# Middle FFN's up projection: block products from its seventh pair on, with the scaled input rewritten by blocks

## The chip, the cores and the metric

One Trainium2 chip, of which the kernel uses one core. The metric is the device time of one execution in microseconds (us). Five engines matter here: TensorE (PE) multiplies matrices, VectorE (DVE) and ScalarE (ACT) work element by element, GpSimd (POOL) does too, and SyncE (SP) issues the loads of the weights. Each engine runs its own instructions in program order and waits for others at semaphores.

## The reference, cut to what matters

The program is two transformer blocks in a row over 512 tokens of width 1024. The second block, `second_block`, begins and ends with a gated feed-forward network. The one in the middle of the whole program (`ffn1`) is the one that changes:

```
h = rms_norm(x, ffn1_norm)
x = x + 0.5 * (silu(h @ w_gate) * (h @ w_up)) @ w_down
```

Here `w_gate` and `w_up` have 2816 columns each, 22 chunks of 128. `ffn2`, the last one, has the same form. All is fp32.

## The kernel before, in words

The activations lie with features on partitions and tokens along the free dimension: `u_hi` and `u_lo` are 8 chunks of 128 features by 512 tokens. Every fp32 value is split into a rounded part (`_hi`, type fp32r) and the rest (`_lo`), and every product is three matmuls: hi by hi, lo by hi, hi by lo.

Weights stream in slabs of 128x1024. SP loads a slab into `raw` (four of them), ACT rounds it into `w_hi` (L1759), POOL subtracts to get `w_lo` (L880), and PE waits for that subtraction before the first matmul of a slab. There are five slab places in `w_hi` and `w_lo`, and ACT's function `feed_to` rounds slabs ahead in its own program order, between its other work.

The three up projections are called `up`, `up1` and `up2`. Each works in 22 pairs: pair c is chunk c of the gate and chunk c of the value. In the plain form a pair is two groups of 8 feature chunks, 48 matmuls of 128x512. So group 2c is pair c's gate and group 2c+1 its value, and group g of `up1` uses slab g of that layer. The first two pairs (four groups) go side by side.

In `up2` the last 18 pairs take another form, which the text calls a block pair. The 1024 by 512 input is cut into 2 by 2 blocks, the pair's weights too, and seven half-size products replace eight (`paired`, 7 products of 12 matmuls, 84 matmuls of 128x256). The products need four sums of input blocks (`s_all`, rounded to `s_hi` on ACT, their rest `s_lo` on POOL), made once, and for every pair seven weight pieces: three raw quarters (pieces 0, 2 and 6), and four differences (pieces 1, 3, 4, 5; in the code `pair_two`, `pair_three`, `pair_one`, `pair_four`). POOL makes the difference of piece 3 (`t_three`, in `slot[5]`) and the rests of pieces 0, 2, 3 and 6. DVE makes the other differences and rests. ACT rounds all seven. Between the products DVE adds partial results (`slot[4]`, `slot[2]`, `slot[3]`, semaphore `st_out`), on which later products of the pair wait; ACT copies the first partial result aside (L2001, semaphore `st_first`) before product 2.

The input of a block pair must be scaled by the norm's factor first, since sums of blocks are taken of it. The layer begins before that factor is known: its first pairs run on the unscaled input, and DVE multiplies their results by the factor `r_sb` (L2675, L2681). In `up2`, DVE scales the input (`scale_input`, L2610), ACT and DVE rewrite `u_hi` and `u_lo`, and DVE makes the block sums (`input_sums`, L2628), all while PE computes the first pairs. In `up1` all 22 pairs are plain, and the input is never scaled.

In both gated layers of the second block, DVE multiplies the silu of the gate by the value (L2684), ACT rounds the product into `a_hi` (L1940) and DVE subtracts to get `a_lo` (L2670). For late chunks of a layer with block pairs the product is kept in `a_kept` instead, and split near the end of the layer.

Of the kernel before, what the change touches and what calls it, by code (L numbers as in the profile page):

```python
# [113 lines left out]
PAIRED = {"up2": (4, FC)}  # L114
# [4 lines left out]
SUM_ORDER = (1, 2, 0, 3)  # L119
# [83 lines left out]
def build(nc, t):  # L203

    ctx = ExitStack()
    with ctx:  # L206
# [609 lines left out]
        def _(pool):  # L816

            def pair_pool(p):

                def low(i, src, hi):  # L820
                    pool.wait_ge(st_hi, hi_no(p, hi))
                    nc.gpsimd.tensor_tensor(piece(w_lo, p, i), src, piece(w_hi, p, i).bitcast(F32),  # L822
                                            ALU.subtract).then_inc(st_pool, 1)

                wait_raw(pool, p, 0)
                wait_raw(pool, p, 1)
                name, c = PAIRS[p]
# [12 lines left out]
                low(6, raw_half(p, 1, 1), 7)  # L840
# [45 lines left out]
        def _(pe):  # L886
# [78 lines left out]
            def dense(name, src_hi, src_lo, k_ready=None, after=None, row=None, row_at=None, again=None, upto=None,  # L965
# [56 lines left out]
                for m in range(ahead, upto or n):  # L1022
                    g = g0 + m
                    wait_bank(g)
                    out = psum[bank_of[g]][:, :]
                    for i in range(k):
                        row_step(m, i)
                        hi, lo = weight(tile)
                        if k_ready and m == 0:
                            pe.wait_ge(k_ready[0], k_ready[1] + i + 1)  # L1030
                        if again is not None and m == ahead:
                            pe.wait_ge(u_ready, again + i + 1)
                        x_hi, x_lo = sources(i)
                        first = mm(out, hi, x_hi, start=(i == 0), stop=False)  # L1034
                        if m == last_reads and i >= 1:
# [9 lines left out]
            def paired(name, scaled):  # L1045
# [17 lines left out]
                for c in range(*PAIRED[name]):  # L1063
# [8 lines left out]
                    if first_pair:  # L1072
                        pe.wait_ge(u_ready, scaled + 4)
# [7 lines left out]
                    if first_pair:  # L1081
                        pe.wait_ge(u_ready, scaled + 8)
# [13 lines left out]
                    pe.wait_ge(st_out, 5 * p + 2)  # L1096
                    product(p, 5, y, "a22", False)
# [621 lines left out]
            dense("up1", u_hi, u_lo, (u_ready, 4 * DC), row="pre2", row_at=(4, 4))  # L1719
            dense("down1", a_hi, a_lo, (a_ready, FC))  # L1720
            dense("wq", u_hi, u_lo, (u_ready, 5 * DC), row="pre3", row_at=(0, 2), again=6 * DC)
# [19 lines left out]
            dense("up2", u_hi, u_lo, (u_ready, 7 * DC), row="pre4", row_at=(0, 2), again=8 * DC, upto=8)  # L1741
            paired("up2", 8 * DC)
# [6 lines left out]
        def _(act):  # L1749
# [186 lines left out]
            def ffn_swiglu(n, name, paired_from=FC, paired_to=FC, unscaled=FC):  # L1936
# [24 lines left out]
                for c in range(paired_from):  # L1961
                    if c == 3 and unscaled == paired_from:
                        for i in range(4):
                            sum_hi_of(name, i)
                    if c == paired_from - 2:
                        pair_raw(p, 0)
                    if c == paired_from - 1:
                        pair_raw(p, 2)
                        pair_three(p)
                        pair_two(p)  # L1970
                        pair_one(p)
                        pair_four(p)
                    silu_of(c)
                    if c == paired_from - 1:
                        pair_raw(p, 6)
                        pair_raw(p + 1, 0)
                        if unscaled == paired_from:
                            for i in range(DC):
                                act.wait_ge(ux_done, DC + 4 + i + 1)
                                if i < DC - 1:  # L1980
                                    act.wait_ge(u_read, DC - 2 + i + 1)
                                else:
                                    act.wait_ge(dense_done, group_of(name, 2 * c + 1))
                                f(u_hi[:, i, :], u_all[:, i, :], ACT.Copy).then_inc(u_part, 1)
                    if 1 <= c <= KEPT_FROM:
                        rounded_a(c - 1)
# [369 lines left out]
            ffn_swiglu(1, "up1")  # L2356
            late_act(3, 24, "mix2", "wq", "down1")
            rewrite_hi(DC + 4, "wq", DC - 2, [slot[4][:, :], slot[5][:, :]])
# [173 lines left out]
            rewrite_hi(2 * DC + 4, "up2", 2 * (DC - 2), [u_all[:, c, :] for c in range(DC)], sums=True)  # L2532
# [5 lines left out]
        def _(dve):  # L2538
# [127 lines left out]
            def ffn_gate(n, name, paired_from=FC, paired_to=FC, unscaled=FC):  # L2666
# [29 lines left out]
                for c in range(paired_from):  # L2696
# [9 lines left out]
                    if c == paired_from - 1 and unscaled == paired_from:  # L2706
                        input_lo(5 * DC)
# [28 lines left out]
                for c in range(paired_from, paired_to):  # L2736
# [17 lines left out]
                    if more:  # L2754
# [11 lines left out]
                    if more:  # L2766
# [4 lines left out]
                    TT(slot[3][:, 0:256], y, kept, ALU.add).then_inc(st_out, 1)  # L2771
                apart(12, 13)
# [433 lines left out]
            ffn_gate(1, "up1")  # L3206
            add_half("down1", 0.5, "pre3", ("mix2", 5 * DC))
            inverse("pre3")
            rewrite("mix2", 6 * DC, r_sb, slot[4:6])
# [190 lines left out]
            add_half("out", 0.5, "pre4", ("ffn2", 7 * DC))  # L3400
            inverse("pre4")
            scale_input("ffn2")
            input_lo(8 * DC)
            input_sums("up2", 3 * DC + 4)
# [162 lines left out]
```

## Time and profile before

| what | value |
|---|---|
| median of 3 runs | 2148.84 us (2148.69 to 2149.2) |
| the profiled execution's own time | 2148.84 us |
| span that its profile shows | 2147.0 us |
| PE busy | 2122.9 us, 99% of the span |
| DVE, ACT, POOL busy | 1009.2, 941.7 and 948.3 us, 44 to 47% |

The span is 1.84 us shorter than the profiled execution's time, which is the median of the runs. A timeline row is: start in us from the span's start, duration in us, engine, line, operation, what it writes and reads, shape, count of instructions merged into the row, and in brackets the idle time of its engine before it and who ended it. PE's matmuls overlap each other, so their pace is read from their starts.

### The profile page before, as it was taken

The page shows a single profiled execution, that of the slowest core. Times are in us where ns is not written, and L with a number is a line of the kernel's source. Part 1 is how long each engine was busy: PE and PEld are TensorE (multiplying, and loading weights), DVE is VectorE, ACT ScalarE, POOL GpSimd, SP SyncE. Part 2 cuts the span into 40 slices and gives each one's busy share as a digit, 9 for nine tenths or more (in the row PEclk, how much of TensorE's full clock was granted, in tenths as well). Part 3 has the DMA queues.
Part 4 walks back from the last instruction along what each step waited for, and adds up shares of the span by engine and source line. Part 5 has one row for each costly group of instructions (what it writes and reads, how often), then busy time and mean ns, then how long its engine had stood idle before and what let it go on. Part 6 is the DMA issues. An engine that isn't in the chain of part 4 may idle for free. (4 is left out here: it accounts for less than half of the span.)

```text
span 2147.0 us, 29183 instructions
## 1 busy us (share of the span) xinstructions
PE 2122.9 (99%) x11584; PEld 1775.0 (83%) x11584; DVE 1009.2 (47%) x1821; ACT 941.7 (44%) x1629; POOL 948.3 (44%) x441
## 2 busy tenths in 40 slices
PE   9999999999999999999999999999999999999998
PEld 8788877787888888888888888778888887999986
DVE  7684555446655400563332124653744127776611
ACT  7835545545544422442223222762346234545521
POOL 4423322345544543654444344143524445766631
PEclk9999999999999999999999999999999999999999
DMA  4313321232332332223333233023322332333321
GB/s 179 97 50 113 112 66 50 104 112 79 108 97 94 114 98 88 89 89 98 98 94 102 89 98 104 21 87 99 111 81 68 98 98 79 99 101 113 117 93 49
DMA packets 56439, 200.68 MB, mean 93 GB/s; under 512 B 6640, under 2 KB 7536, under 8 KB 55920
## 3 DMA queue, kind: packets, MB, share of 16 engines
q1 hardware_dynamic: 52416, 188.77, 27.7%
q10 hardware_dynamic: 3888, 10.05, 1.4%
q8 instruction: 92, 1.51, 0.3%
q14 instruction: 43, 0.35, 0.1%
HBM read 194.60 MB, written 2.10 MB: 92 GB/s over the span
## 5 line engine op out<-in xcount | busy, mean ns | idle before, releaser
L880 POOL TENSOR_TENSOR w_lo<-raw,w_hi 128x1024 fp32r<-128x1024 f32 x313 | 770.0, 2472 | 1013.6 <-ACT w_hi L1759 985.7
L1759 ACT ACTIVATE w_hi<-raw 128x1024 fp32r<-128x1024 f32 x316 | 326.7, 1051 | 146.9 <-PE dense L1038 84.7
L1034 PE MATMUL dense<-u_hi,w_hi 128*128 128x512 f32 x608 | 237.4, 391 | 0.6 <-ACT slot L1950 0.6
L1038 PE MATMUL dense<-u_hi,w_lo 128*128 128x512 f32 x608 | 236.6, 389 | 0.0
L1037 PE MATMUL dense<-u_lo,w_hi 128*128 128x512 f32 x584 | 227.2, 389 | 0.0
L1034 PE MATMUL dense<-a_hi,w_hi 128*128 128x512 f32 x400 | 156.0, 390 | 0.0
L1037 PE MATMUL dense<-a_lo,w_hi 128*128 128x512 f32 x400 | 155.6, 389 | 0.0
L1038 PE MATMUL dense<-a_hi,w_lo 128*128 128x512 f32 x400 | 155.6, 389 | 0.0
L1034 PE MATMUL misc<-u_hi,w_hi 128*128 128x512 f32 x368 | 143.6, 390 | 0.7 <-DVE u_lo L2616 0.7
L1038 PE MATMUL misc<-u_hi,w_lo 128*128 128x512 f32 x368 | 143.2, 389 | 0.0
L1037 PE MATMUL misc<-u_lo,w_hi 128*128 128x512 f32 x360 | 140.1, 389 | 0.0
L1034 PEld LDWEIGHTS dense<-u_hi,w_hi 128*128 128x128 f32 x608 | 114.1, 188 | 25.3 <-ACT slot L1950 1.1
L1038 PEld LDWEIGHTS dense<-u_hi,w_lo 128*128 128x128 f32 x608 | 114.1, 188 | 23.8
L1037 PEld LDWEIGHTS dense<-u_lo,w_hi 128*128 128x128 f32 x584 | 109.6, 188 | 22.8
L2784 DVE SCALAR_TENSOR_TENSOR h<-dense,h 128x512 f32<-128x512 f32 x24 | 16.6, 692 | 212.9 <-PE dense L1038 212.9
L822 POOL TENSOR_TENSOR w_lo<-raw,w_hi 128x512 fp32r<-128x512 f32 x54 | 70.1, 1313 | 56.2 <-ACT w_hi L1765 56.2
L1037 PEld LDWEIGHTS dense<-a_lo,w_hi 128*128 128x128 f32 x400 | 75.1, 188 | 15.9 <-issue 0.2
L1034 PEld LDWEIGHTS dense<-a_hi,w_hi 128*128 128x128 f32 x400 | 75.1, 188 | 15.7 <-issue 0.2
L1038 PEld LDWEIGHTS dense<-a_hi,w_lo 128*128 128x128 f32 x400 | 75.1, 188 | 15.5
L1034 PEld LDWEIGHTS misc<-u_hi,w_hi 128*128 128x128 f32 x368 | 69.1, 188 | 15.8 <-issue 1.5
L958 PE MATMUL misc<-u_hi,w_hi 128*128 128x512 f32 x192 | 81.6, 425 | 0.0
L1038 PEld LDWEIGHTS misc<-u_hi,w_lo 128*128 128x128 f32 x368 | 69.1, 188 | 14.5
(569 smaller groups left out, 5009.3 us busy)
## 6 DMA issues: line engine op xcount, KB each, us to landing
raw<-in_weights SPq DMA_DIRECT2D x352, 512.0 KB, 3.5
h<-in_x SPq DMA_DIRECT2D x4, 512.0 KB, 6.6
alibi<-in_alibi ACTq DMA_DIRECT2D x1, 2048.0 KB, 8.9
h<-in_x ACTq DMA_DIRECT2D x2, 1024.0 KB, 7.2
out<-result SPq DMA_DIRECT2D x8, 256.0 KB, 2.2
p_raw<-in_p ACTq DMA_DIRECT2D x2, 512.0 KB, 3.2
hn<-mqk ACTq DMA_DIRECT2D x4, 256.0 KB, 4.0
mqk<-mqk ACTq DMA_DIRECT2D x4, 256.0 KB, 3.9
```

Of the source, the lines that this page charges most:

```text
L822: nc.gpsimd.tensor_tensor(piece(w_lo, p, i), src, piece(w_hi, p, i).bitcast(F32), ALU.subtract).then_inc(st_pool, 1)
L880: nc.gpsimd.tensor_tensor(w_lo[:, ring(s), :, :], raw[:, s % RAWS, :, :], w_hi[:, ring(s), :, :].bitcast(F32), ALU.subtract).then_inc(w_sp ...
L958: mm(out, hi, src_hi[:, i, :], start=(i == 0), stop=False)
L1034: first = mm(out, hi, x_hi, start=(i == 0), stop=False)
L1037: mm(out, hi, x_lo, start=False, stop=False)
L1038: last = mm(out, lo, x_hi, start=False, stop=(i == k - 1))
L1759: f(w_hi[:, ring(s), :, :], raw[:, s % RAWS, :, :], ACT.Copy).then_inc(w_part, 1)
L2784: STT(h[:, c, :], out_bank(name, c)[:, :], scale, h[:, c, :], ALU.mult, ALU.add).then_inc(h_ready, 1)
```

## The change

The layer `up1` joins `PAIRED`, from pair 6 on: its pairs 0 to 5 stay plain and pairs 6 to 21 become block pairs. What comes with that:

- DVE's `ffn_gate` scales the whole input after pair 1 and makes the block sums after pair 2. ACT's `ffn_swiglu` rounds the four sums after the silu of pair 3.
- The input is rewritten in three blocks, at the end of pair 5: features 0 to 511 of the first 256 tokens (block a11), then features 512 to 1023 of the first and of the second 256 tokens (a12, a22). PE waits for each at the product that reads it first.
- In the first block pair of `up1` DVE takes another order (`late`): the value of pair 5, and the weight differences of the next pair one at a time between the additions.
- POOL's first block pair of a layer, in `up1` and in `up2` alike, takes the four rests of the sums in turns with the weight pieces, where `up2` had them all ahead of the weight pieces.
- ACT rounds the activation of an earlier pair before it rounds the weight pieces of the first block pair.
- `down1` takes the turned order of sources and the banks that `down2` has.

```diff
-PAIRED = {"up2": (4, FC)}
+PAIRED = {"up1": (6, FC), "up2": (4, FC)}
...
-                if c == PAIRED[name][0]:
-                    for i in SUM_ORDER:
-                        pool.wait_ge(st_hi, sum_no(name, i + 1, BLOCKS))
-                        nc.gpsimd.tensor_tensor(s_lo[i][:, :, :], s_all[:, i, :, :], s_hi[i][:, :, :].bitcast(F32),
-                                                ALU.subtract).then_inc(st_slo, 1)
-                else:
+                if not first_pair:
                     pool.wait_ge(st_pool, 5 * p - 1)
                 three = t_three[:, :].rearrange("p (a b) -> p a b", a=4)
                 nc.gpsimd.tensor_tensor(three, raw_half(p, 1, 1), raw_half(p, 1, 0), ALU.subtract).then_inc(st_pool, 1)
                 low(0, raw_half(p, 0, 0), 1)
+                if first_pair:
+                    sum_low(1)
                 low(2, raw_half(p, 0, 1), 2)
+                if first_pair:
+                    sum_low(2)
                 low(3, three, 3)
+                if first_pair:
+                    sum_low(0)
+                    sum_low(3)
                 low(6, raw_half(p, 1, 1), 7)
...
-            dense("up1", u_hi, u_lo, (u_ready, 4 * DC), row="pre2", row_at=(4, 4))
-            dense("down1", a_hi, a_lo, (a_ready, FC))
+            dense("up1", u_hi, u_lo, (u_ready, 4 * DC), row="pre2", row_at=(4, 4), upto=12, last_reads=11)
+            paired("up1", 5 * DC + 1, 5 * DC + 2, 5 * DC + 3)
+            dense("down1", a_hi, a_lo, (a_ready, FC), turned_from=KEPT_FROM)
...
                     if c == paired_from - 1:
+                        if c <= KEPT_FROM:
+                            rounded_a(c - 1)
                         pair_raw(p, 2)
                         pair_three(p)
                         pair_two(p)
                         pair_one(p)
                         pair_four(p)
                     silu_of(c)
+                    if c == 3 and unscaled == paired_from:
+                        for i in range(4):
+                            sum_hi_of(name, i)
                     if c == paired_from - 1:
                         pair_raw(p, 6)
+                        if unscaled == paired_from:
+                            act.wait_ge(ux_done, 2 * DC + 4)
+                            act.wait_ge(u_read, DC - 1)
+                            f(u_hi[:, 0:4, 0:256], u_all[:, 0:4, 0:256], ACT.Copy).then_inc(u_part, 1)
+                            act.wait_ge(dense_done, group_of(name, 2 * c + 1))
+                            for x in (slice(0, 256), slice(256, S)):
+                                f(u_hi[:, 4:8, x], u_all[:, 4:8, x], ACT.Copy).then_inc(u_part, 1)
...
                     if c == paired_from - 1 and unscaled == paired_from:
-                        input_lo(5 * DC)
+                        low_a(c - 1)
+                        for i, (k, x) in enumerate(((0, slice(0, 256)), (4, slice(0, 256)), (4, slice(256, S)))):
+                            dve.wait_ge(u_part, 5 * DC + i + 1)
+                            TT(u_lo[:, k:k + 4, x], u_all[:, k:k + 4, x], u_hi[:, k:k + 4, x].bitcast(F32),
+                               ALU.subtract).then_inc(u_ready, 1)
+                        break
...
                     TT(slot[4][:, 0:256], y, kept, ALU.add).then_inc(st_out, 1)
-                    if more:
+                    late = c == paired_from == unscaled
+                    if late:
+                        value_of(c - 1)
+                    elif more:
                         pair_one(p + 1)
                         pair_two(p + 1)
...
-            ffn_gate(1, "up1")
+            ffn_gate(1, "up1", *PAIRED["up1"], PAIRED["up1"][0])
```

The order of instructions moves at three places.

On ACT in `up1`, between the silu of pair 3 (it writes `slot1` from `dense0`) and that of pair 4. Before:

```order
L1950 ACTIVATE slot1_62<-dense0 128x512 [waits a_ready,up_scaled]
L1940 ACTIVATE a_hi_142<-slot0_61 128x512 [waits a_raw]
L1759 ACTIVATE w_hi_50<-raw_49 128x1024 [waits dense_done,w_loaded1]
L1759 ACTIVATE w_hi_50<-raw_49 128x1024 [waits dense_done,w_loaded2]
L1950 ACTIVATE slot0_61<-dense2 128x512 [waits a_ready,up_scaled]
```

With the change:

```order
L1961 ACTIVATE slot1_62<-dense0 128x512 [waits a_ready,up_scaled]
L1808 ACTIVATE s_hi0_147<-s_all_146 128x1024 [waits st_diff]
L1808 ACTIVATE s_hi1_148<-s_all_146 128x1024 [waits st_diff]
L1808 ACTIVATE s_hi2_149<-s_all_146 128x1024 [waits st_diff]
L1808 ACTIVATE s_hi3_150<-s_all_146 128x1024 [waits st_diff]
L1951 ACTIVATE a_hi_142<-slot0_61 128x512 [waits a_raw]
L1776 ACTIVATE w_hi_50<-raw_49 128x512 [waits dense_done,w_loaded3]
L1770 ACTIVATE w_hi_50<-raw_49 128x1024 [waits dense_done,w_loaded1]
L1770 ACTIVATE w_hi_50<-raw_49 128x1024 [waits dense_done,w_loaded2]
L1961 ACTIVATE slot0_61<-dense2 128x512 [waits a_ready,up_scaled]
```

The two whole slabs are those of groups 10 and 11. They now stand behind the four sums and one weight quarter of the first block pair.

On DVE in `up1`, from the product of pair 1 (`slot1` by `dense3`) to the gate of pair 3 (`dense0`). Before:

```order
L2684 TENSOR_TENSOR slot1_62<-slot1_62,dense3 128x512 [waits up_act,dve_step]
L2670 TENSOR_TENSOR a_lo_143<-slot0_61,a_hi_142 128x512 [waits a_part]
L2675 TENSOR_TENSOR misc0<-misc0,r_sb_155 128x512 [waits dense_done]
L2681 TENSOR_TENSOR misc1<-misc1,r_sb_155 128x512 [waits dense_done]
L2684 TENSOR_TENSOR slot0_61<-slot0_61,misc1 128x512 [waits up_act,dve_step]
L2670 TENSOR_TENSOR a_lo_143<-slot1_62,a_hi_142 128x512 [waits a_part]
L2675 TENSOR_TENSOR dense0<-dense0,r_sb_155 128x512 [waits dense_done]
```

With the change:

```order
L2696 TENSOR_TENSOR slot1_62<-slot1_62,dense3 128x512 [waits up_act,dve_step]
L2622 SCALAR_TENSOR_TENSOR u_all_145<-h_52,vec_56,r_sb_155 128x512 x8
L2682 TENSOR_TENSOR a_lo_143<-slot0_61,a_hi_142 128x512 [waits a_part]
L2687 TENSOR_TENSOR misc0<-misc0,r_sb_155 128x512 [waits dense_done]
L2693 TENSOR_TENSOR misc1<-misc1,r_sb_155 128x512 [waits dense_done]
L2696 TENSOR_TENSOR slot0_61<-slot0_61,misc1 128x512 [waits up_act,dve_step]
L2640 TENSOR_TENSOR s_all_146<-u_all_145 128x1024 [waits ux_done]
L2640 TENSOR_TENSOR s_all_146<-s_all_146,u_all_145 128x1024 [waits st_diff]
L2640 TENSOR_TENSOR s_all_146<-u_all_145 128x1024
L2640 TENSOR_TENSOR s_all_146<-u_all_145,s_all_146 128x1024 [waits st_diff]
L2682 TENSOR_TENSOR a_lo_143<-slot1_62,a_hi_142 128x512 [waits a_part]
L2687 TENSOR_TENSOR dense0<-dense0,r_sb_155 128x512 [waits dense_done]
```

The gate of pair 3, on which ACT's silu of pair 3 waits, now stands behind eight scalings and four sums.

On POOL at the start of `up2`'s block pairs, from the end of the plain slabs to the difference `slot5` of the second block pair (pair 5). Before:

```order
L831 TENSOR_TENSOR s_lo1_152<-s_all_146,s_hi1_148 128x1024 [waits st_hi,w_loaded3,w_loaded2]
L831 TENSOR_TENSOR s_lo2_153<-s_all_146,s_hi2_149 128x1024 [waits st_hi]
L831 TENSOR_TENSOR s_lo0_151<-s_all_146,s_hi0_147 128x1024 [waits st_hi]
L831 TENSOR_TENSOR s_lo3_154<-s_all_146,s_hi3_150 128x1024 [waits st_hi]
L836 TENSOR_TENSOR slot5_66<-raw_49 128x512
L822 TENSOR_TENSOR w_lo_51<-raw_49,w_hi_50 128x512 [waits st_hi] x2
L822 TENSOR_TENSOR w_lo_51<-slot5_66,w_hi_50 128x512 [waits st_hi]
L822 TENSOR_TENSOR w_lo_51<-raw_49,w_hi_50 128x512 [waits st_hi]
L836 TENSOR_TENSOR slot5_66<-raw_49 128x512 [waits st_pool,w_loaded1,w_loaded0]
```

With the change:

```order
L837 TENSOR_TENSOR slot5_66<-raw_49 128x512 [waits w_loaded3,w_loaded2]
L821 TENSOR_TENSOR w_lo_51<-raw_49,w_hi_50 128x512 [waits st_hi]
L831 TENSOR_TENSOR s_lo1_152<-s_all_146,s_hi1_148 128x1024 [waits st_hi]
L821 TENSOR_TENSOR w_lo_51<-raw_49,w_hi_50 128x512 [waits st_hi]
L831 TENSOR_TENSOR s_lo2_153<-s_all_146,s_hi2_149 128x1024 [waits st_hi]
L821 TENSOR_TENSOR w_lo_51<-slot5_66,w_hi_50 128x512 [waits st_hi]
L831 TENSOR_TENSOR s_lo0_151<-s_all_146,s_hi0_147 128x1024 [waits st_hi]
L831 TENSOR_TENSOR s_lo3_154<-s_all_146,s_hi3_150 128x1024 [waits st_hi]
L821 TENSOR_TENSOR w_lo_51<-raw_49,w_hi_50 128x512 [waits st_hi]
L837 TENSOR_TENSOR slot5_66<-raw_49 128x512 [waits st_pool,w_loaded1,w_loaded0]
```

The first difference moved to the head, and every rest of a sum now stands behind the rest of piece 0, which waits for ACT to round that piece.

## Rows read from the trace of the kernel before

**Rows 1.** The page: busy time by engine, and TensorE's granted clock in 40 slices.

```profile
PE 2122.9 (99%) x11584; PEld 1775.0 (83%) x11584; DVE 1009.2 (47%) x1821; ACT 941.7 (44%) x1629; POOL 948.3 (44%) x441
PEclk9999999999999999999999999999999999999999
```

**Rows 2.** Timeline of PE in `up1`: first matmuls of groups 10 and 11.

```profile
970.19 0.39 PE L1034 MATMUL misc<-u_hi,w_hi 128*128 128x512 f32 x1
...
975.63 0.39 PE L1034 MATMUL misc<-u_hi,w_hi 128*128 128x512 f32 x1
```

**Rows 3.** Timeline of PE in `up2`'s block pairs: first matmuls of pairs, and waits.

```profile
1829.67 0.28 PE L1058 MATMUL dense<-u_hi,w_hi 128*128 128x256 f32 x1
...
1833.84 0.36 PE L1058 MATMUL dense<-u_hi,w_hi 128*128 128x256 f32 x1 [1.13 <-POOL w_lo L822]
...
1840.18 0.35 PE L1058 MATMUL misc<-s_hi,w_hi 128*128 128x256 f32 x1 [0.36 <-issue]
...
1841.68 0.28 PE L1058 MATMUL misc<-u_hi,w_hi 128*128 128x256 f32 x1
...
1850.88 0.36 PE L1058 MATMUL dense<-s_hi,w_hi 128*128 128x256 f32 x1 [0.41 <-DVE slot L2765]
...
1862.47 0.28 PE L1058 MATMUL misc<-u_hi,w_hi 128*128 128x256 f32 x1
...
1872.55 0.28 PE L1058 MATMUL dense<-u_hi,w_hi 128*128 128x256 f32 x1
...
2011.28 0.36 PE L1058 MATMUL dense<-u_hi,w_hi 128*128 128x256 f32 x1 [0.33 <-DVE slot L2753]
```

**Rows 4.** Timeline of DVE in `up1`, from the factor on.

```profile
942.63 0.70 DVE L2675 TENSOR_TENSOR dense<-dense,r_sb 128x512 f32<-128x512 f32 x1 [5.29 <-ACT r_sb L1934]
...
947.25 0.68 DVE L2670 TENSOR_TENSOR a_lo<-slot,a_hi 128x512 fp32r<-128x512 f32 x1
```

**Rows 5.** Timeline of ACT in `up1`.

```profile
949.60 1.05 ACT L1759 ACTIVATE w_hi<-raw 128x1024 fp32r<-128x1024 f32 x1
954.80 0.60 ACT L1950 ACTIVATE slot<-dense 128x512 f32<-128x512 f32 x1 [4.15 <-DVE dense L2675]
...
955.82 2.00 ACT L1759 ACTIVATE w_hi<-raw 128x1024 fp32r<-128x1024 f32 x2
```

**Rows 6.** Timeline of DVE at the start of `up2`.

```profile
1813.22 1.22 DVE L2628 TENSOR_TENSOR s_all<-u_all 128x1024 f32<-128x1024 f32 x1
...
1823.02 2.90 DVE L2639 TENSOR_TENSOR misc<-raw 128x512 f32<-128x512 f32 x1
...
1837.33 0.68 DVE L2655 TENSOR_TENSOR w_lo<-misc,w_hi 128x512 fp32r<-128x512 f32 x1
1838.11 0.70 DVE L2650 TENSOR_TENSOR misc<-raw,misc 128x512 f32<-128x512 f32 x1
1838.72 1.03 DVE L2670 TENSOR_TENSOR a_lo<-slot,a_hi 128x512 fp32r<-128x512 f32 x1
```

**Rows 7.** Timeline of POOL at the start of `up2`.

```profile
1814.57 10.79 POOL L831 TENSOR_TENSOR s_lo<-s_all,s_hi 128x1024 fp32r<-128x1024 f32 x4 [8.42 <-ACT s_hi L1797]
...
1833.23 1.74 POOL L836 TENSOR_TENSOR slot<-raw 128x512 f32<-128x512 f32 x1
...
1842.54 2.57 POOL L822 TENSOR_TENSOR w_lo<-raw,w_hi 128x512 fp32r<-128x512 f32 x2
```

**Rows 8.** Timeline of ACT at the start of `up2`.

```profile
1821.03 0.62 ACT L1765 ACTIVATE w_hi<-raw 128x512 fp32r<-128x512 f32 x1
...
1833.36 0.38 ACT L2001 ACTIVATE slot<-dense 128x256 f32<-128x256 f32 x1
1835.00 0.63 ACT L1765 ACTIVATE w_hi<-slot 128x512 fp32r<-128x512 f32 x1 [1.26 <-POOL slot L836]
```

**Rows 9.** DVE's line that scales the input: duration ns as min/median/max.

```profile
L2610 DVE SCALAR_TENSOR_TENSOR u_all<-h,vec,r_sb x8: 739/750/2905, 1790.3 to 1801.4; 128x512 f32<-128x512 f32 x8
```

**Rows 10.** POOL's line for a plain slab: duration ns as min/median/max.

```profile
L880 POOL TENSOR_TENSOR w_lo<-raw,w_hi x313: 2340/2399/3311, 7.4 to 2109.0; 128x1024 fp32r<-128x1024 f32 x157
```

More of the change, by code:

```diff
@@ L118 @@
 SUM_AT = (2, 0, 1, 3)
-SUM_ORDER = (1, 2, 0, 3)
 def first_slab(name, c):
@@ L1034, in dense @@
                         first = mm(out, hi, x_hi, start=(i == 0), stop=False)
-                        if m == last_reads and i >= 1:
+                        if m == last_reads and i == 4:
                             first.then_inc(u_read, 1)
@@ L1096, in paired @@
                     pe.wait_ge(st_out, 5 * p + 2)
+                    if first_pair:
+                        pe.wait_ge(u_ready, a22_ready)
                     product(p, 5, y, "a22", False)
@@ L1740, in _ @@
             dense("out", mg_hi, mg_lo, (mg_ready, 0))
-            dense("up2", u_hi, u_lo, (u_ready, 7 * DC), row="pre4", row_at=(0, 2), again=8 * DC, upto=8)
-            paired("up2", 8 * DC)
+            dense("up2", u_hi, u_lo, (u_ready, 7 * DC + 3), row="pre4", row_at=(0, 2), again=8 * DC + 3, upto=8)
+            paired("up2", 8 * DC + 7, 8 * DC + 11, 8 * DC + 11)
             dense("down2", a_hi, a_lo, (a_ready, 2 * FC), row="pre5", row_at=(DC - 1, FC - 2), turned_from=KEPT_FROM)
@@ L1961, in ffn_swiglu @@
                 for c in range(paired_from):
-                    if c == 3 and unscaled == paired_from:
-                        for i in range(4):
-                            sum_hi_of(name, i)
                     if c == paired_from - 2:
@@ L1973, in ffn_swiglu @@
                     silu_of(c)
+                    if c == 3 and unscaled == paired_from:
+                        for i in range(4):
+                            sum_hi_of(name, i)
                     if c == paired_from - 1:
                         pair_raw(p, 6)
-                        pair_raw(p + 1, 0)
[L1977 to L1985, printed above, removed]
+                        if unscaled == paired_from:
[5 more added lines that the diff above has]
+                                f(u_hi[:, 4:8, x], u_all[:, 4:8, x], ACT.Copy).then_inc(u_part, 1)
+                        pair_raw(p + 1, 0)
+                    elif 1 <= c <= KEPT_FROM:
                         rounded_a(c - 1)
@@ L2355, in _ @@
             late_act(2, 16, "ffn1", "up1")
-            ffn_swiglu(1, "up1")
+            ffn_swiglu(1, "up1", *PAIRED["up1"], PAIRED["up1"][0])
             late_act(3, 24, "mix2", "wq", "down1")
-            rewrite_hi(DC + 4, "wq", DC - 2, [slot[4][:, :], slot[5][:, :]])
+            rewrite_hi(2 * DC + 4, "wq", DC - 1, [slot[4][:, :], slot[5][:, :]])
             act.dma_start(wvb[:, :], t["wvb"]).then_inc(c_loaded, 16)
@@ L2531, in _ @@
             late_act(4, 32, "ffn2", "up2", "out")
-            rewrite_hi(2 * DC + 4, "up2", 2 * (DC - 2), [u_all[:, c, :] for c in range(DC)], sums=True)
+            rewrite_hi(3 * DC + 4, "up2", 2 * DC - 3, [u_all[:, c, :] for c in range(DC)], sums=True)
             ffn_swiglu(2, "up2", *PAIRED["up2"], 2)
@@ L2753, in ffn_gate @@
                     TT(slot[4][:, 256:S], y, kept, ALU.add).then_inc(st_out, 1)
-                    if more:
+                    if late:
+                        pair_one(p + 1)
+                    elif more:
                         pair_two_lo(p + 1)
@@ L2765, in ffn_gate @@
                     TT(slot[2][:, 256:S], z, slot[4][:, 256:S], ALU.add).then_inc(st_out, 1)
-                    if more:
+                    if late:
+                        pair_two(p + 1)
+                    elif more:
                         pair_four_lo(p + 1)
@@ L2771, in ffn_gate @@
                     TT(slot[3][:, 0:256], y, kept, ALU.add).then_inc(st_out, 1)
+                    if late:
+                        pair_two_lo(p + 1)
+                        pair_four(p + 1)
+                        pair_four_lo(p + 1)
                 apart(12, 13)
@@ L3205, in _ @@
             inverse("pre2")
-            ffn_gate(1, "up1")
-            add_half("down1", 0.5, "pre3", ("mix2", 5 * DC))
+            ffn_gate(1, "up1", *PAIRED["up1"], PAIRED["up1"][0])
+            add_half("down1", 0.5, "pre3", ("mix2", 5 * DC + 3))
             inverse("pre3")
-            rewrite("mix2", 6 * DC, r_sb, slot[4:6])
+            rewrite("mix2", 6 * DC + 3, r_sb, slot[4:6])
             for c in range(8):
@@ L3399, in _ @@
                 TT(mg_lo[:, m, :], ma[:, m, :], mg_hi[:, m, :].bitcast(F32), ALU.subtract).then_inc(mg_ready, 1)
-            add_half("out", 0.5, "pre4", ("ffn2", 7 * DC))
+            add_half("out", 0.5, "pre4", ("ffn2", 7 * DC + 3))
             inverse("pre4")
             scale_input("ffn2")
-            input_lo(8 * DC)
-            input_sums("up2", 3 * DC + 4)
+            input_lo(8 * DC + 3)
+            input_sums("up2", 4 * DC + 4)
             ffn_gate(2, "up2", *PAIRED["up2"], 2)
```

13 lines of the change are left out of this document (9 added, 4 removed).

## Prediction, made before the changed kernel ran

> **What bounds the kernel now.** I read the page first: PE is busy for 99% of the span, and its granted clock is at full speed, 2.4 GHz, in every slice [rows 1]. So only two things can change the time: the sum of PE's own pace, and new waits of PE. Then I read PE's timeline in `up1`, the layer that changes, for its pace: a group of 24 matmuls goes from 970.19 to 975.63, which is 5.44 us or 226.7 ns a matmul, and a plain pair takes 10.88 us [rows 2]. Then I read PE's timeline in `up2`, which already has block pairs. Undisturbed, a pair goes from 1862.47 to 1872.55: 10.08 us for 84 matmuls, 120 ns each [rows 3]. The reader should see there that the first pairs do not reach this: the first takes 12.01 us (1829.67 to 1841.68), with restarts at 1833.84 (product 2) and 1840.18 (product 6). The second waits once (1850.88) and so does the last (2011.28) [rows 3]. Last I read DVE, ACT and POOL around both places, since a layer that enters block pairs asks much of these three in a short time, and each works strictly in program order.
>
> **What is removed.** Sixteen pairs go from 10.88 to 10.08 us: 16 x 0.80 = 12.8 us [rows 2, 3]. The Trainium skill ("TensorE: Matmul & The Clock Gate", section on the back-to-back issue gap) gives N/2.4 + 2.5 ns for a matmul of N columns on a warm engine. By that page a plain pair would be an estimated 10.36 us and a block pair 9.17, and sixteen would give 19 us. No row here has either pace, and the sum goes by the rows. Also gone are DVE's multiplications by the factor for these pairs, off PE's path.
>
> **Added wait 1: the slab of group 10.** I carry the times of the trace on. DVE is free for the scaling at 947.25 [rows 4]. POOL has nothing to do then, since ACT's next slab now comes only after the silu of pair 2. Eight scalings at 0.75 us [rows 9], less about 0.08 each for overlap with the next start, end at 952.6. A rest, the gate and the value of pair 2 (four operations of some 0.7 us [rows 4]) end at 955.3. Then come four block sums of 1.22 us [rows 6], about 4.8 us. But ACT's slab of group 9 now starts at 955.0 and POOL's 2.40 us for it [rows 10] fall into these sums. When both engines read SBUF only, one waits for the other: the first difference on DVE at 1823.02 took 2.90 us [rows 6], while POOL's first operations took 1.74 us where the later ones go in 2.57 for two [rows 7]. So I add 2.0 us, and with one more rest and the gate of pair 3 DVE is at 963.35. ACT follows with the silu (0.60), four roundings of the sums at some 1.0, two half-size ones at 0.5 and the slab of group 10 at 1.05 [rows 5, 8]: 969.85. POOL's 2.40 us end at 972.3. PE wanted group 10 at 970.19 [rows 2]. That is 2.1 us, plus 0.1 for the restart: **2.2 us**. The bounds are 0.2 (POOL's slab beside the sums costs nothing) and 2.8.
>
> **Added wait 2: the first block pair of `up1`.** Group 11 now ends at 981.07 + 2.2 = 983.3. Until then the chain is: POOL's slab of group 11 to 974.9, its first difference to 976.6 (1.74 [rows 7], beside a rest of DVE); ACT rounds pieces 3 and 1 (977.7); DVE's rest and difference 5, 0.7 each [rows 6]; ACT rounds it (979.7); DVE's rest and the gate of pair 5 (981.1); ACT's silu, one quarter, and then block a11 of the input, 1.05, ready at 983.2. The rest of a11 on DVE takes 1.22 alone, and 2 us behind one of POOL's, which has the rests of the sums in hand then. Product 0 starts at 985.2, **1.9 late** (bounds 1.2 and 2.4). After it DVE has a12 and a22, each behind an operation of POOL (1.25, then 2.4), then a rest of a weight piece and the first addition, for which product 3 waits: about 991.8, where 985.2 + 36 x 0.12 = 989.5 would do. **2.3 late** (bounds 0 and 3).
>
> **Added waits 3: second and last pair.** `late` leaves the next pair's piece 1, 5 and 4 to the end of the first pair. By the same count the first addition of pair 7 comes 0.65 late, about what the second pair of `up2` lost (1850.88 [rows 3]); bounds 0 and 2. The last pair has the code of `up2`'s last, and I take its wait: the gap before 2011.28 cost some 0.6 [rows 3].
>
> **POOL's turns, in `up2` too.** Before, POOL did the four rests of the sums from 1814.57 to 1825.36, while ACT was still busy with pairs 0 and 1 [rows 7]. Now they stand behind the rest of piece 0, and ACT rounds piece 0 at 1821.03 to 1821.65 [rows 8], after two silus and an activation; nothing in the change moves that. So POOL makes its first difference early and then stands idle until 1821.7. From there it has four rests of sums (2.36 each, between the shortest and the median of a plain slab [rows 10]) and, to the end of the second pair's difference, five half-size operations (1.25 from start to start): 15.7 us, and 1.9 more for four collisions with DVE at 0.45 (1.74 less 1.3 [rows 7]). It ends at 1839.3. Before, that second difference ended at 1833.23 + 1.74 = 1834.97 [rows 7].
>
> What waits for it: ACT rounds it (at 1835.00 in the trace [rows 8]), and behind that row stand an activation, the silu and piece 1 of the second pair. DVE then has the rest of piece 1, difference 5, a rest of an activation, and only then the addition that product 6 of the first pair waits for [rows 6]. From the end of that difference to product 6 the trace has 1840.18 - 1834.97 = 5.2 us [rows 3, 7]. Some 0.4 of it was a wait for PE, so I take 4.8. Product 6 starts at 1844.1 and the pair ends 12 x 0.12 later, 1845.5, against 1841.68: **3.9 us lost**. In return the early difference cures the wait at 1833.84, which the view puts on POOL, but which ended with ACT's copy at 1833.36 + 0.38 [rows 3, 8]; that is in these numbers already. Bounds: no collisions and 4.6 us of chain give 1.8; the full 5.2 and one more collision give 4.9. I take 3.9, since collisions are the rule in these rows.
>
> **The sum.** -12.8 + 2.2 + 1.9 + 2.3 + 0.65 + 0.6 + 3.9 = -1.2 us. The span of 2147.0 becomes 2145.8; with the 1.84 us around it 2147.6, and the profiled execution is the median, so **2147.6 us** it is for the median too. The turned sources and banks of `down1`, the counts of the later layers, and the loads cost nothing: the same instructions stand there, and two slabs per 10.08 us are what `up2` streams. ACT's earlier activation is in the chains above.
>
> **Rivals.** Measured against no change, 0.2% (4.3 us) is about what the measurement can tell.
>
> *POOL's turns do not hold `up2` up.* If product 6 came on time, `up2` would lose nothing and gain its 1.9 us of first waits: -12.8 + 7.7 - 1.9 = -7.0, 2141.8 us. It needs the second difference by about 1833.5; the order of POOL's rows speaks against it. A kin of it is that the collisions hardly count, on both layers: lower bounds 0.2 + 1.2 + 0 + 0 + 0.6 and 1.8 give -9.0, 2139.8. Together 0.33.
>
> *`up1` never catches up, and the kernel is slower.* DVE begins the second block pair behind. If every further pair of `up1` kept the 0.65 us of the second, 14 x 0.65 = 9.1 us come on top: 2156.7. The point from which it decides is whether DVE needs over 10.08 us for a pair's work. Against it: `up2` is in step from its third pair on [rows 3]. For it: the first pair hands on more work than in `up2`. Chance 0.12.
>
> *A block pair at the page's pace.* The Trainium skill's rule for the gap (the same section) would make the gain 19 us. As a mechanism of this kernel it would mean that block matmuls in `up1` start every 109 ns and plain ones every 216, which gives -19 + 11.6 = -7.4, 2141.4 us. `up2`'s identical matmuls at 120 ns leave it 0.02.
>
> **The numbers.** The forecast's case has 0.53, and its own range is 2144.5 to 2151, where the waits' upper bounds (0.6, 1.2, 1.35 and 1.0 us more) would not all meet. The range for 8 in 10 reaches down into the first rival, 2140.5, and up to 2152. Faster by over 0.2% (below 2144.5) 0.36, within 0.2% 0.50, slower (above 2153.1) 0.14.
>
> **What would show it.** Block pairs of `up1` from its third on at 10.08 us; a gap of PE before group 10 that ends with POOL's slab; gaps before products 0 and 3 of the first block pair, ended by DVE's rest of the input and first addition; in `up2`, POOL idle before 1821.7 on the old axis, no gap before product 2, and one of some 6 us before product 6. I am wrong if PE does not stop before group 10 or product 6, or if later pairs of `up1` stop too.

## The result, and the profile after

The changed kernel takes 2152.34 us (median of 15 runs, 2151.67 to 2154.07), the kernel before 2149.2 us on the same chip: a ratio of 1.0015, 95% interval 1.0008 to 1.0022. That is 3.1 us slower, where the forecast of 2147.6 us was a little faster, and 0.3 us above its range. By the bound of 0.2% it is no change.

The page of the changed kernel, by engine (busy us, share of the span, instructions):

```profile
PE 2115.0 (98%) x12160; PEld 1795.3 (83%) x12160; DVE 1105.2 (51%) x1996; ACT 987.2 (46%) x1748; POOL 993.6 (46%) x493
```

PE is busy for 7.9 us less than in [rows 1], so the block products do save work; the waits took more than that back. PE's timeline in `up1`, first matmul behind each wait (start, duration, and in brackets the idle time and who ended it):

```profile
973.79 0.47 PE L1042 MATMUL misc<-u_hi,w_hi 128*128 128x512 f32 x1 [1.52 <-POOL w_lo L888]
...
986.59 0.36 PE L1066 MATMUL dense<-u_hi,w_hi 128*128 128x256 f32 x1 [1.67 <-DVE u_lo L2722]
993.05 0.36 PE L1066 MATMUL dense<-s_hi,w_hi 128*128 128x256 f32 x1 [1.91 <-issue]
1003.08 0.36 PE L1066 MATMUL misc<-u_hi,w_hi 128*128 128x256 f32 x1 [1.17 <-ACT slot L2013]
...
1149.08 0.36 PE L1066 MATMUL dense<-u_hi,w_hi 128*128 128x256 f32 x1 [0.33 <-DVE slot L2773]
```

These are, in order, group 10, product 0 and product 3 of the first block pair, product 2 of the second and product 2 of the last. Between the second and the last, each pair takes 10.08 us. The same for `up2`, from the second group of its start to the second block pair:

```profile
1806.14 0.51 PE L1042 MATMUL misc<-u_hi,w_hi 128*128 128x512 f32 x1 [0.67 <-DVE u_lo L2628]
...
1836.94 0.28 PE L1068 MATMUL dense<-u_hi,w_lo 128*128 128x256 f32 x1
1842.84 0.55 PE L1066 MATMUL misc<-s_hi,w_hi 128*128 128x256 f32 x1 [5.62 <-POOL w_lo L821]
1843.19 0.42 PE L1067 MATMUL misc<-s_lo,w_hi 128*128 128x256 f32 x1
1843.41 0.42 PE L1068 MATMUL misc<-s_hi,w_lo 128*128 128x256 f32 x1
```

No wait stands ahead of product 2 any more (1833.84 in [rows 3]), and a wait of 5.6 us stands ahead of product 6. Behind it the starts lie 213 ns apart, not 120. The table of windows shows why (length, PE busy and its matmuls, granted clock as a share of 2.4 GHz, DMA):

```profile
1836.90:1842.80 5.90, 0.32 (x3) 0.86 0.31 95
1842.80:1848.00 5.20, 5.16 (x24) 0.50 0.57 195
1848.10:1853.00 4.90, 4.90 (x43) 1.00 0.02 3
```

In the wait the granted clock falls to 0.50, its level of 1.2 GHz (half clock, below), and it stays there for 24 matmuls. The page's row of the clock in 40 slices shows 9 throughout, as in [rows 1]: 5 us vanish in a slice of 54. The Trainium skill ("TensorE: Matmul & The Clock Gate", section on HAM oscillation) says that an engine left idle between bursts of matmuls comes back at half rate; this trace agrees, with 0.50 behind 5.6 us.

What held product 6 is read from POOL, ACT and DVE:

```profile
1803.80 1.74 POOL L837 TENSOR_TENSOR slot<-raw 128x512 f32<-128x512 f32 x1
1820.52 1.42 POOL L821 TENSOR_TENSOR w_lo<-raw,w_hi 128x512 fp32r<-128x512 f32 x1 [14.98 <-ACT w_hi L1776]
1821.90 2.85 POOL L831 TENSOR_TENSOR s_lo<-s_all,s_hi 128x1024 fp32r<-128x1024 f32 x1
...
1830.04 5.67 POOL L831 TENSOR_TENSOR s_lo<-s_all,s_hi 128x1024 fp32r<-128x1024 f32 x2
1835.66 1.31 POOL L821 TENSOR_TENSOR w_lo<-raw,w_hi 128x512 fp32r<-128x512 f32 x1
1836.91 1.28 POOL L837 TENSOR_TENSOR slot<-raw 128x512 f32<-128x512 f32 x1
```

```profile
1838.22 0.63 ACT L1776 ACTIVATE w_hi<-slot 128x512 fp32r<-128x512 f32 x1 [7.74 <-POOL slot L837]
```

```profile
1842.33 0.41 DVE L2787 TENSOR_TENSOR slot<-misc,slot 128x256 f32<-128x256 f32 x1
```

POOL stands idle for 15 us behind its first difference, does the sums afterwards, and comes to the second pair's difference at 1836.91. ACT rounds that at 1838.22, and DVE's addition for product 6 ends at 1842.74. The view names POOL, but POOL's rest of piece 6 had ended at 1836.97 (1835.66 + 1.31). DVE's addition ended 0.1 us before product 6 started, so that addition, at the end of POOL's chain, is what was late.

The start of `up2` lost too. At 1803.80 POOL's first difference meets DVE's rests of the input (L2628), and the group at 1806.14 waits for one of them. The second rest takes 1.77 us beside POOL, and those behind it 0.68. Below is DVE's row there, merged over four rests, 5.38 us:

```profile
1801.91 5.38 DVE L2628 TENSOR_TENSOR u_lo<-u_all,u_hi 128x512 fp32r<-128x512 f32 x4 [2.09 <-ACT u_hi L1873]
```

Against the trace before, PE's starts are 1.95 us later when `up1` begins, 3.03 earlier at `down1`, 2.51 earlier at `wq`'s second group, 2.31 earlier at `up2` and 4.55 later at its third block pair. The 1.95 arise ahead of `up1`: 1.5 of them are matmuls at half clock behind a 1.9 us wait at 222 us. The ten profiles of the experiments have that wait too, one of them with 2.2 us, and none has the half clock there.

### The profile page after: what moved, and what is told of

The parts are those of the page before. It is cut to its first block and busy times, and to the rows that moved or that the text cites. A ratio compares the mean times of both kernels' runs of the same rounds, so it can differ in the third digit from the quotient of the medians.

```text
span 2151.6 us, 30943 instructions
## 1 busy us (share of the span) xinstructions
PE 2115.0 (98%) x12160; PEld 1795.3 (83%) x12160; DVE 1105.2 (51%) x1996; ACT 987.2 (46%) x1748; POOL 993.6 (46%) x493
## 5 line engine op out<-in xcount | busy, mean ns | idle before, releaser
L888 POOL TENSOR_TENSOR w_lo<-raw,w_hi 128x1024 fp32r<-128x1024 f32 x281 | 695.6, 2487 | 920.1 <-ACT w_hi L1770 892.3
L821 POOL TENSOR_TENSOR w_lo<-raw,w_hi 128x512 fp32r<-128x512 f32 x102 | 131.4, 1302 | 116.1 <-ACT w_hi L1776 116.1
L1042 PE MATMUL dense<-u_hi,w_hi 128*128 128x512 f32 x432 | 168.9, 391 | 0.8 <-ACT slot L1961 0.8
L1046 PE MATMUL dense<-u_hi,w_lo 128*128 128x512 f32 x432 | 168.1, 389 | 0.0
L1045 PE MATMUL dense<-u_lo,w_hi 128*128 128x512 f32 x408 | 158.7, 389 | 0.0
L1066 PE MATMUL dense<-s_hi,w_hi 128*128 128x256 f32 x408 | 115.7, 284 | 2.0 <-issue 1.9
L1042 PE MATMUL misc<-u_hi,w_hi 128*128 128x512 f32 x288 | 112.7, 391 | 2.9 <-POOL w_lo L888 1.5
L1067 PE MATMUL dense<-s_lo,w_hi 128*128 128x256 f32 x408 | 115.4, 283 | 0.0
L1068 PE MATMUL dense<-s_hi,w_lo 128*128 128x256 f32 x408 | 115.4, 283 | 0.0
L1046 PE MATMUL dense<-a_lo,w_lo 128*128 128x512 f32 x256 | 99.6, 389 | 0.0
```

The costliest lines, as they stand in the source:

```text
L888: nc.gpsimd.tensor_tensor(w_lo[:, ring(s), :, :], raw[:, s % RAWS, :, :], w_hi[:, ring(s), :, :].bitcast(F32), ALU.subtract).then_inc(w_sp ...
L1066: mm(out, hi[:, k, :], a_h[:, k, :], start=(start and k == 0), stop=False, skip_group_check=True)
L1067: mm(out, hi[:, k, :], a_l[:, k, :], start=False, stop=False, skip_group_check=True)
L1068: last = mm(out, lo[:, k, :], a_h[:, k, :], start=False, stop=(k == 3), skip_group_check=True)
```

## The experiments

Theory: `up1` does what was forecast, and POOL's turns in `up2` cost more than forecast, by the half clock behind the wait (2.25 us) and by the collision at the start of `up2` (0.95). Rivals: the clock fell for a reason of its own, or the wait comes from the new code in general and not from POOL's order. All ratios are to the kernel before, which had 2149.19 to 2149.33 us beside them.

**Old order in `up2`.**

```diff
+                turns = first_pair and name == "up1"
                 if not first_pair:
                     pool.wait_ge(st_pool, 5 * p - 1)
+                elif not turns:
+                    for i in (1, 2, 0, 3):
+                        sum_low(i)
...
-                if first_pair:
+                if turns:
                     sum_low(1)
```

> The changed kernel with POOL's order of before in up2 alone (its four sum remainders ahead of the first difference); up1 keeps the turns. Theory (POOL's turns in up2 cost 0.95 us at the start of up2, about 3.6 us of a longer wait at product 6 of the first block pair and 2.25 us of matmuls at half clock behind that wait): 2145.6 us, product 2 of that pair waits again, product 6 hardly, and no stretch at a granted clock of 0.50. Rival A (the clock falls there for another reason than the wait): 2147.9. Rival B (the wait at product 6 is due to the new code around up1 and the sums, not to the order on POOL): 2152.

Measured: 2145.87 us, ratio 0.9983 (0.9974 to 0.9991), 6.5 us below the changed kernel. The waits of PE in `up2` (total, times, longest):

```profile
PE dense L1070 <- POOL w_lo L821: 1.3, 1, 1.3
PE misc L1070 <- issue: 0.8, 1, 0.8
PE misc L1046 <- DVE u_lo L2632: 0.7, 1, 0.7
PE dense L1046 <- ACT slot L1965: 0.6, 1, 0.6
```

Product 2 waits again and product 6 for 0.8 us only; DVE's rests take 5.49 us for six where the changed kernel had 5.38 for four. So the theory holds for `up2`, and with POOL's old order there the change is 3.3 us faster than the kernel before.

**The turns alone.** The kernel before, with the new `pair_pool` and nothing else.

```diff
-                if c == PAIRED[name][0]:
-                    for i in SUM_ORDER:
...
+                if first_pair:
+                    sum_low(1)
                 low(2, raw_half(p, 0, 1), 2)
```

> The kernel before with POOL's turns in up2 and nothing else of the change. Theory: it loses what up2 lost in the changed kernel, 0.95 + 5.8 us, so 2155.9 us against 2149.2, with the same 5.6 us wait at product 6 and the same stretch at half clock. Rival A (the start of up2 was late because of the phase in which the changed kernel reaches it, not because of POOL's early difference): 2155.0. Rival B (the turns cost little by themselves): 2149 to 2150.

Measured: 2155.0 us, ratio 1.0028 (1.0018 to 1.0039), 5.8 us slower. Its trace loses 1.07 us from `up2`'s first matmul to its first block pair, 5.11 in that pair, and gets 0.22 back in the second. The time is Rival A's number, but the start of `up2` does lose what Rival A excludes; the theory's 2155.9 was 0.9 too high in all. Here the half clock ends after some 14 matmuls where the changed kernel had 24 (columns as above):

```profile
1844.60:1848.00 3.40, 3.05 (x14) 0.51 0.68 195
```

**No idle time ahead of product 6.** Added matmuls fill the wait, into a bank that nobody reads.

```diff
                     product(p, 5, y, "a22", False)
+                    if first_pair and name == "up2":
+                        idle = pair_banks(p + 1)[2]
+                        pe.wait_ge(*last_before_pairs[name][idle])
+                        spare = psum[idle][:, 0:256]
+                        for _ in range(42):
+                            mm(spare, piece(w_hi, p, 5)[:, 0, :], u_hi[:, 4, second], start=True, stop=True,
+                               skip_group_check=True)
```

> The changed kernel, and in the wait ahead of product 6 of up2's first block pair PE runs 42 matmuls of 128x256 into a bank that nobody reads (42 x 0.120 = 5.0 us of a wait of 5.6 us). They compute nothing that is used. Theory (the granted clock falls to 0.50 because PE stands idle): product 6 starts as late as before, 14.4 us after its pair, but its matmuls and those behind it run at 1.00 and the time is 2.2 us less than that of the changed kernel, 2150.1. Rival A (the clock falls at that place whatever PE does): no gain, 2152.3. Rival B (PE's extra reads slow POOL or DVE down, or the 42 matmuls end later than the wait): 2152.5 or more.

Measured: 2150.39 us, ratio 1.0005 (0.9997 to 1.0014), 1.95 us below the changed kernel. Product 6 starts 14.51 us after its pair, 0.1 later than in the changed kernel, and the window behind it shows:

```profile
1841.20:1846.40 5.20, 5.10 (x42) 1.00 0.56 196
```

42 matmuls where the changed kernel had 24. This experiment took nothing away but PE's idleness, so the idleness is what brought the half clock, and neither rival holds. From the first pair's start to the third's, the trace takes 26.4 us instead of 28.5. All five profiles with a wait of 5.6 us there and no added matmuls (the changed kernel, the turns alone and the next three with POOL's turns in `up2`) have half clock behind it, for 14 to 30 matmuls.

**`down1`'s banks of before.**

```diff
-        for name in PAIRED:
-            for m in range(DC):
-                bank_of[START["down" + name[2:]][1] + m] = (2, 3, 0, 1)[m % 4]
+        for m in range(DC):
+            bank_of[START["down2"][1] + m] = (2, 3, 0, 1)[m % 4]
```

> The changed kernel with down1's groups in the banks of before (0, 1, 2, 3 in turn), down2's as they are. Theory (the last groups of down1 now share banks with the first groups of wq): the first wq groups start 0.5 us earlier against down1, 2151.8 us. Rival (the start of wq hangs on DVE's late input alone, whatever the banks): 2152.3, no difference. Either difference is near what five rounds can tell; the trace's step from down1 to wq decides.

Measured: 2151.72 us, ratio 1.0010 (1.0001 to 1.0018), 0.6 us below, near what the runs can tell. `wq`'s first group starts as before, 119.7 us after `down1`. The gap ahead of its second group is gone, so that one comes 0.5 us earlier (first the changed kernel, then this one; the second row of each is that group):

```profile
1272.05 0.39 PE L1018 MATMUL dense<-u_hi,w_lo 128*128 128x512 f32 x1
1272.77 0.50 PE L1015 MATMUL dense<-u_hi,w_hi 128*128 128x512 f32 x1 [0.33 <-DVE h L2812]
```

```profile
1270.46 0.39 PE L1017 MATMUL dense<-u_hi,w_lo 128*128 128x512 f32 x1
1270.69 0.39 PE L1014 MATMUL dense<-u_hi,w_hi 128*128 128x512 f32 x1
```

**ACT's slabs first.** In `up1`, ACT rounds the slabs of groups 10 and 11 ahead of the four sums.

```diff
                     if c == 3 and unscaled == paired_from:
+                        feed(name, 2 * c + 4)
                         for i in range(4):
                             sum_hi_of(name, i)
```

> The changed kernel with ACT rounding the slabs of up1's groups 10 and 11 ahead of the four input sums, not behind them. Theory (group 10 waits because POOL's remainder of its slab waits for ACT's rounding, which stands behind 4.2 us of sums): group 10 starts 1.6 us earlier against up1's start, and since nothing behind it was late before, the time falls by 0.5 to 1.6 us, to 2150.7 to 2151.8. Rival (ACT then waits for a free place in the ring, and the sums and DVE's work behind them come late): no gain or a loss, 2152 to 2154.

Measured: 2152.37 us, no gain. Group 10 starts 1.69 us earlier against the start of `up1`, and product 0 waits for 4.53 instead of 1.67, so that it starts 1.1 us later. The sums, and the rounding for which DVE waits behind them, come 1.9 us later on ACT. And POOL is through with its slabs sooner, so its first rest of the block pair meets DVE's first difference (POOL, then DVE):

```profile
970.82 1.76 POOL L821 TENSOR_TENSOR w_lo<-raw,w_hi 128x512 fp32r<-128x512 f32 x1
```

```profile
971.35 1.78 DVE L2652 TENSOR_TENSOR misc<-raw 128x512 f32<-128x512 f32 x1
...
973.77 0.69 DVE L2688 TENSOR_TENSOR dense<-dense,r_sb 128x512 f32<-128x512 f32 x1
```

That difference took 0.69 us in the changed kernel. With both losses the gate at 973.77 comes 3.7 us later, of which slack takes up all but the 1.1. The longer wait was also followed by half clock (columns as above):

```profile
986.00:989.50 3.50, 3.48 (x16) 0.51 0.00 0
```

Product 3 then waits for 0.4 us instead of 1.9, and `up1` takes 236.3 us in all, where the changed kernel took 235.9. The rival holds in its outcome. Of its mechanism, the later sums are there and no wait of ACT for a free slab place is; the collision and the half clock it did not name.

**DVE's third rest later.** The rest of a22 is moved behind the first addition (in the code it is item 2 of the loop over the three rests), the value of pair 5 behind the second.

```diff
                     if late:
-                        value_of(c - 1)
+                        low_u(2)
...
                     if late:
+                        value_of(c - 1)
                         pair_one(p + 1)
```

> The changed kernel with DVE's third input remainder of up1's first block pair moved behind the first sum of outputs, and the value of pair 5 behind the second. Theory (product 3 waits 2.2 us for that sum, which stands behind 3.4 us of the third remainder): product 3 waits at most 0.3 us, product 5 waits for the third remainder some 0.3 us in its place, and the time falls by 1.5 to 2 us, to 2150.5. Rival (the third remainder, which product 5 needs, takes over the wait at its full length): 2152.3.

Measured: 2151.74 us, 0.6 us below the changed kernel, a third of what the theory had. The traces don't put those 0.6 down to the edit: `up1` takes 236.0 us, 0.1 more than in the changed kernel. Product 3's wait is gone, 2.07 us, and 2.0 of new waits stand behind it:

```profile
PE dense L1066 <- DVE u_lo L2710: 1.7, 1, 1.7
PE misc L1042 <- POOL w_lo L888: 1.6, 1, 1.6
PE misc L1066 <- ACT slot L2013: 1.5, 1, 1.5
PE misc L1066 <- POOL w_lo L821: 1.4, 2, 1.1
```

The last row is product 6 and the second pair's first product, and the third the second pair's product 2. POOL works without a pause up to there, so what comes earlier waits for POOL instead. In `up1` the outcome is the rival's, at other products than the one it named.

**Old order in both layers.** The edit of the first experiment, with `turns` false throughout.

> The changed kernel with POOL's four sum remainders ahead of the first difference in up1 as well as in up2. Theory (in up1 POOL's first piece, for which product 0 waits, is then late by the four remainders, about 2.5 us beyond the time when DVE's input remainder is ready, while product 3 is relieved because DVE no longer collides with POOL there): between 2145 and 2148, against 2145.9 with the turns kept in up1. Rival (the turns are worth their place in up1, since everything behind POOL's first piece moves with it): 2148.5 or more.

Measured: 2153.8 us, ratio 1.0019 (1.0011 to 1.0028), 7.9 us above the kernel with turns in `up1`; the rival holds, and more than it had. POOL does the four sums in one go and product 0 waits for 10.5 us:

```profile
975.32 9.88 POOL L831 TENSOR_TENSOR s_lo<-s_all,s_hi 128x1024 fp32r<-128x1024 f32 x4
985.16 1.26 POOL L841 TENSOR_TENSOR slot<-raw 128x512 f32<-128x512 f32 x1
```

```profile
994.78 0.55 PE L1070 MATMUL dense<-u_hi,w_hi 128*128 128x256 f32 x1 [10.47 <-DVE u_lo L2726]
```

I had counted POOL's own piece, not ACT, which waits for the difference at 985.16 ahead of the input's first quarter. The 28 matmuls behind the wait ran at a granted clock of 0.50, which is part of the loss. In the traces `up1` takes 244.7 us, and 236.7 with the turns.

**Four edits together** (old order in `up2`, banks, slabs first, third rest later).

> The changed kernel with four edits together: POOL's old order in up2 alone, down1's banks of before, ACT's slabs of groups 10 and 11 ahead of the sums, and DVE's third input remainder behind the first sum of outputs. Theory (the four losses are at four different places and add up): 2152.3 - 6.5 - 0.5 - 1.0 - 1.9 = 2142.4 us, faster than both kernels. Rival (what is gained ahead of up1's first block pair is waited for again at its products, since POOL's first pieces don't come earlier): 2145 us.

Measured: 2146.63 us, ratio 0.9987 (0.9978 to 0.9996): 0.8 above the first edit alone, and above both the theory's number and the rival's. The longer wait at product 0 that the slabs bring was followed by 23 matmuls at a granted clock of 0.50, and `up1` takes 237.5 us.

**Three edits** (the same without ACT's slabs), and **a fourth** in their place: ACT rounds a11 ahead of pair 5's silu.

```diff
+                    if c == paired_from - 1 and unscaled == paired_from:
+                        act.wait_ge(ux_done, 2 * DC + 4)
+                        act.wait_ge(u_read, DC - 1)
+                        f(u_hi[:, 0:4, 0:256], u_all[:, 0:4, 0:256], ACT.Copy).then_inc(u_part, 1)
                     silu_of(c)
```

> The changed kernel with three edits: POOL's old order in up2 alone, down1's banks of before, and DVE's third input remainder behind the first sum of outputs; ACT's order stays. Theory (these three add up, and the fourth edit, ACT's slabs first, was what cost e8 its gain): 2145.9 - 0.5 - 0.4 = 2145.0 us, and up to 1.4 us less where the wait of product 3 in up1 was followed by half clock, so 2143.6 to 2145.0. Rival (the edits in up1 only move the wait, as the slabs did): 2146.

> The kernel of the three edits, and ACT rounds the first quarter of up1's scaled input as soon as group 11 has read it, ahead of pair 5's SiLU and of the piece for product 6. Theory (product 0 waits 1.7 us for DVE's remainder of that quarter, which waits for ACT, which stands 1.4 us behind these two): product 0 starts 1.2 to 1.4 us earlier and the time is 1 us below that of the three edits. Rival (POOL, which works through from 976 to 996 us, then holds product 4 or 6 for as much longer): the same time as the three edits.

Measured: 2144.96 us, ratio 0.9981 (0.9972 to 0.9990), with three; 2145.07 us, the same ratio, with four. Three edits make the fastest kernel of the study, 4.4 us below before and 7.4 below the changed one. The theory's number holds for the three, but not as a gain inside `up1`, which takes 236.1 us. Against the trace of the first edit alone (236.7) it lacks the half clock behind product 3, and the banks bring their 0.5 at `wq`. The fourth moved nothing: the time is its rival's, but no product waits longer, since product 0 itself starts hardly sooner, at 985.66 against 985.71. DVE starts the rest of a11 0.9 us earlier, meets POOL's sum, and ends when it did (DVE with three, DVE with four, POOL with four, merged over two rests on DVE):

```profile
983.57 4.22 DVE L2713 TENSOR_TENSOR u_lo<-u_all,u_hi 128x1024 fp32r<-128x1024 f32 x2 [1.35 <-ACT u_hi L1995]
```

```profile
982.68 5.06 DVE L2714 TENSOR_TENSOR u_lo<-u_all,u_hi 128x1024 fp32r<-128x1024 f32 x2 [0.50 <-ACT u_hi L1989]
```

```profile
981.58 2.85 POOL L830 TENSOR_TENSOR s_lo<-s_all,s_hi 128x1024 fp32r<-128x1024 f32 x1
```

The Trainium skill ("SBUF — State Buffer", section on who interferes with whom) says that when both read SBUF, DVE with two inputs there, the second to start blocks until the first is through. The rows agree: POOL's sum ends at 984.43 with four and at 984.48 with three, and DVE's two rests end at 987.79 and 987.74 (983.57 + 4.22, 982.68 + 5.06), though they start 0.9 us apart.

## Why the prediction missed

| term of the sum | forecast | measured in the trace |
|---|---|---|
| pace of 16 pairs | -12.8 | -12.8 (10.08 us a pair) |
| group 10's slab | +2.2 | +1.7 |
| product 0 of `up1`'s first block pair | +1.9 | +1.9 |
| product 3 | +2.3 | +2.1, and 0.1 in restarts |
| second pair | +0.65 | +1.4, at product 2 |
| last pair | +0.6 | +0.5 |
| `down1`, to `wq`'s first groups | 0 | +0.5 |
| `wq` to `up2` | 0 | +0.2 |
| start of `up2` | 0 | +1.1 |
| first block pair of `up2` | +3.9 | +5.1 |
| second block pair of `up2` | 0 | +0.7 |
| sum (measured: 4.55 - 1.95; the rounded terms give 2.5) | -1.2 | +2.6 |

The step that failed is "POOL's turns, in `up2` too". Its mechanism was right to the end: POOL idle until ACT rounds piece 0, the second difference late, no wait before product 2, and product 6 at 14.4 us after its pair's start, where the forecast also had 14.4. What it put at nothing is what follows a long wait: "the pair ends 12 x 0.12 later" took full speed for granted. The third experiment shows that PE's idleness brings the half clock, and that it costs 2.1 us over the first two pairs. The same step took POOL's early difference as free; it stands where DVE makes the input's rests, and the first two experiments show the loss of 1.1 us vanish and appear with POOL's order. Together the step cost 6.9 us, not 3.9: 3.0 of the 4.7 us between 2147.6 and 2152.34. Its upper bound of 4.9 did not reach that either, and by its own terms the bound is 4.7 (1839.3 + 0.45 + 5.2 + 1.44 against 1841.68); four collisions at 0.45 are 1.8, not 1.9. Another 0.4 of the 4.7 is the kernel before, which took 2149.2 us in these runs and not 2148.84.

The sentence that `down1`'s banks cost nothing was wrong by 0.5 us, which the fourth experiment takes back in the trace, though its time alone would not prove it. The second pair of `up1` was forecast, by `up2`, to wait for the first addition; it waited for ACT's copy of the first partial result, and the size was off by 0.7. The four other waits of `up1` hold within 0.5 us. That its total comes out within 0.2 is partly luck: group 10 was 0.5 too dear and the second pair 0.7 too cheap.

Of the rivals, the first (POOL's turns do not hold `up2` up) is refuted. The second (`up1` never catches up) is too: from the third pair to the last but one nothing is lost, and the layer takes 5.0 us less than before. The third is refuted as well: 10.08 us for 84 matmuls is 120 ns each, not 109.

What stays open: the 0.5 us between the sum of the trace and the medians, and the remaining waits of `up1`'s entry. Three edits there (slabs first, third rest later, a11 sooner) moved waits without making the layer shorter. That POOL's work and its collisions with DVE set the bound is read from rows, not tested by taking work from POOL.

## What to carry to other kernels

A wait of several microseconds on PE is priced with what comes behind it: add the matmuls that run at half clock, or give PE something harmless to do, which here delayed product 6 by 0.1 us and saved 2.1. An order that suits one layer need not suit its twin: the turns are worth 7.9 us in `up1`, where POOL comes late, and cost 6.5 in `up2`, where POOL was idle when the sums were ready. Where DVE and POOL share a stretch, starting one earlier only moves the collision; count which operation it will meet.

## What the hardware showed

A wait need not be long for the clock to fall, and the same wait does not always bring it down. Product 3 of `up1`'s first block pair started 2.2 us after the matmul before it both in the changed kernel and in the one with the old order in `up2`. The first then ran at 1.00, and so did the kernels without idle time and with the old banks, behind the same 2.2 us. The one with the old order had this behind it (columns as above):

```profile
991.30:994.80 3.50, 3.45 (x17) 0.55 0.00 0
```

Up to the second pair that cost 1.5 us, of which a shorter wait in that pair gave back 0.7. What decides it is not shown. Whether such events make the spread between runs of one kernel was not tried.
